# Turning the FFN input before its norm's root, and scaling each up piece by a row of roots on VectorE

## Chip, cores and metric

The kernel runs on one core of a Trainium2 chip. The metric is the device time of one execution in microseconds; lower is better.

## What is computed

The kernel is a two-layer encoder trunk over 256 tokens of width 1024. Each layer has an attention sublayer and then a gated MLP with a depthwise convolution of width 3 over the tokens. Only the MLP (the FFN) and the norm ahead of it are touched here:

```python
D_MODEL, SEQ, DEPTH, D_FF, CONV_WIDTH = 1024, 256, 2, 2816, 3

def rms_norm(x, g):
    y = x * lax.rsqrt(jnp.mean(x * x, axis=-1, keepdims=True) + NORM_EPS)
    return y * g

def conv_gated_mlp(h, w_up, conv_w, w_down):
    u = h @ w_up                                  # (tokens, 5632)
    up = jnp.pad(u, ((0, 0), (1, 1), (0, 0)))
    u = sum(up[:, t:t + S] * conv_w[t] for t in range(3))
    gate, val = jnp.split(u, 2, axis=-1)
    return (jax.nn.gelu(gate, approximate=True) * val) @ w_down

# in each layer, after the attention sublayer:
x = x + rms_norm(merged @ w_out, attn_post_norm)
h = rms_norm(x, ffn_pre_norm)
x = x + rms_norm(conv_gated_mlp(h, w_up, ffn_conv, w_down), ffn_post_norm)
```

## The kernel before

**Products in three passes.** Every large product is made of two rounded parts of each operand: a high part and a low part (`value - high`). `passes` (L1352) issues three matmuls for each 128-row step of the contraction: high by low, low by high, high by high (L1354 to L1356).

**Weights in pieces.** Weights come in pieces of at most 128x2048, in the order that `plan_pieces` writes out, through rings of 3 slots (`RING`). For each piece SP issues the DMA into `raw` when the low part of the piece three places earlier is done, ScalarE writes the high part (`split_hi`, L685 to L691), VectorE the low part (`split_lo`, L1030 to L1035), and TensorE uses it (`use_piece`, L1411). ScalarE may write a slot only when TensorE has finished the piece that held it (`piece_used`). Each engine walks the same list of steps (`STEPS`) in order. At step ("w", n) ScalarE and VectorE first split piece n + 2, then do what is due on piece n's result.

**The FFN.** It has NU = 11 units of 256 channels. For unit u there are two up pieces, number c = 2u (gate half) and c = 2u + 1 (value half), each 8 contraction steps by 2 channel blocks by 3 passes = 48 matmuls over 256 tokens, written into bank 4 + c % 4 with channels on partitions and tokens on the free axis. The down piece of unit u follows two units later (`LAG`), 24 matmuls of 512 columns. So the order is up 0 to up 5, down 0, up 6, up 7, down 1, and so on to up 20, up 21, down 8, down 9, down 10. On each up result:

- ScalarE multiplies the two blocks of the bank by the middle tap into `conv` (L930);
- VectorE adds the left tap and the right tap, two instructions each, reading the bank again (L1304, L1310);
- after the value half ScalarE takes Gelu of the gate half (L937), VectorE multiplies value by Gelu (L1316), ScalarE writes the high part of the product, `g_hi` (L942), and VectorE its low part, `g_lo` (L1318). The two wait for each other in turn. TensorE's down piece waits for `g_lo`.

**Between attention and FFN (the "mid" step, L854, L1231, L1669).** The output product `out` ends with a tile for each of the two token halves t. For each, ScalarE squares and sums the second 512 columns (`post_square`), GpSimd takes the root (`root`), VectorE multiplies by the gain and adds to `x` (`post_gained`, `post_add` L1187). Then the FFN's own norm follows: ScalarE squares `x` (`pre_square` L835), GpSimd takes the root, and VectorE writes `xn = x * root` (`pre_scale` L1073). TensorE turns `xn` by transposes (`turn_ffn` L1563), ScalarE writes the high part times the norm's gain (`ffn_hi` L803), VectorE the low part (`ffn_lo` L1062, in the order of `FFN_LO`), and up 0 begins. Between the two halves TensorE does `MID_WAIT` = 24 idle transposes (`keep_clock`, L1333).

Of the kernel before, what the change touches and what calls it, by code (L numbers as in the profile page):

```python
# [8 lines left out]
F32 = mybir.dt.float32  # L9
# [3 lines left out]
ALU = mybir.AluOpType  # L13
# [3 lines left out]
P = 128  # L17
# [27 lines left out]
MID_WAIT = 24  # L45
# [4 lines left out]
G_RING = 3  # L50
# [219 lines left out]
FFN_LO = [(0, 0), (0, 1), (1, 0), (1, 1), (0, 2), (1, 2), (0, 3), (1, 3)]  # L270
# [21 lines left out]
def build_trunk(nc, a, out):  # L292
    with ExitStack() as ctx:
# [73 lines left out]
        with ExitStack() as four:  # L367
# [3 lines left out]
            square_ffn = sb("square_ffn", [P, D], scope=four)  # L371
        with ExitStack() as six:
            sb("pad_six", [P, 5120], scope=six)
            par_rows = sb("par_rows", [44, 4 * DEPTH, P], scope=six)
# [40 lines left out]
        ffn_squares, xn_done = sem("ffn_squares"), sem("xn_done")  # L415
# [80 lines left out]
        def turned_bank(t, k):  # L496

            return bank[((0, 1, 6, 7), (2, 3, 0, 1))[t][k // 2]][:, (k % 2) * P:(k % 2 + 1) * P]
# [165 lines left out]
        def _(act):  # L664
# [150 lines left out]

            def pre_attn(l):
# [22 lines left out]
            for l in range(DEPTH):  # L839
                for step in STEPS:  # L840
# [13 lines left out]
                    elif what == "mid":  # L854
# [59 lines left out]
                    elif what == "w":  # L914
# [7 lines left out]
                        if kind == "up":  # L922
                            u, b = c // 2, c % 2
                            act.wait_ge(piece_used, l * NPIECE + (RING + n + 1))
                            if u >= 2:

                                act.wait_ge(g_lo_done, l * NU + (u - 1))
                            for j in range(2):
                                ch = 22 * b + 2 * u + j
                                last = nc.scalar.activation(conv[:, u % 2, b, j * SEQ:(j + 1) * SEQ],  # L930
                                                            bank[4 + c % 4][:, j * SEQ:(j + 1) * SEQ], ACT.Copy,
                                                            scale=par_all[:, l, 44 + ch:45 + ch])
                            last.then_inc(conv_mid, 1)
                            if c % 2 == 1:
# [3 lines left out]
                                act.wait_ge(g_ready, l * NU + (u + 1))  # L938
                                if u >= G_RING:

                                    act.wait_ge(piece_used, l * NPIECE + (RING + PIECES.index(("down", u - G_RING, 0, 2, 1024)) + 1))
                                nc.scalar.activation(by_class2(g_hi[:, u % G_RING, :]), own_order2(conv[:, u % 2, 1, :]), ACT.Copy).then_inc(g_hi_done, 1)  # L942
# [8 lines left out]
        def _(dve):  # L951
# [115 lines left out]
            def pre_scale(l, t):  # L1067
# [3 lines left out]
                for h in range(2):  # L1071
                    s = slice(h * 512, h * 512 + 512)
                    V.tensor_scalar(xn[:, t, s], x[:, t, s], roots[:, j:j + 1], None, ALU.mult).then_inc(xn_done, 1)  # L1073
# [675 lines left out]
```

## Time and profile before

| | |
|---|---|
| median of 3 runs | 1039.35 us (1038.99 to 1039.72) |
| the profiled execution | 1039.12 us |
| its span in the trace | 1037.0 us |
| TensorE matmul busy | 1015.7 us, 98% |
| VectorE busy | 658.0 us, 63% |
| ScalarE busy | 583.5 us, 56% |
| granted TensorE clock, mean | 0.998 |
| HBM traffic | 164 GB/s over the span |

The span is what the trace covers; 2.1 us of the profiled execution's time lie around it. Lines like L1062 are lines of the kernel before. The start of an interval is counted in microseconds from the start of the span. Where a row of the timeline says `[1.74 <-DVE x_normed L1073]`, the engine stood idle for 1.74 us before it, and what ended the idle time was that VectorE instruction.

### The profile page before, as it was taken

Reading aid. Unit: us, or ns where it says so; the run is one execution under the profiler, and the core shown is the slowest. Engines: PE = TensorE matmul, PEld = TensorE weight load, DVE = VectorE, ACT = ScalarE, POOL = GpSimd, SP = SyncE. Lnnn points to the kernel's source line nnn. Section 1 sums busy time; section 2 is a strip of 40 time slices with the busy share of each in tenths; the row PEclk is TensorE's granted clock in tenths of the full one; section 3 lists DMA queues with packets and bytes.
Section 4 is the critical chain, followed back from the end, with each engine's and each line's share of the span. In section 5 each row is a group of like instructions: output and inputs, shape, how many; then the busy total and the mean of one; then the engine's idle time right before and its main releaser. Section 6 shows DMA issues by size and latency. Waiting matters only on the chain.

```text
span 1037.0 us, 15899 instructions
## 1 busy us (share of the span) xinstructions
PE 1015.7 (98%) x6256; PEld 911.2 (88%) x6256; DVE 658.0 (63%) x886; ACT 583.5 (56%) x859; POOL 129.3 (12%) x257
## 2 busy tenths in 40 slices
PE   8999999999998999999999999999999989999997
PEld 7889999888877999999988899998888789999996
DVE  5636566655586776776765355656555878777675
ACT  5657666556445555454575666665553456545452
POOL 3353114000001000000024321220000010000000
PEclk9999999999999999999999999999999999999999
DMA  8555445444444654645455544465445444554541
GB/s 252 182 179 153 126 143 172 146 160 162 143 160 144 203 198 153 219 160 206 138 177 163 172 123 127 148 203 163 133 152 182 163 144 166 188 215 163 203 162 41
DMA packets 106222, 170.79 MB, mean 165 GB/s; under 512 B 3377, under 2 KB 72804, under 8 KB 106148
## 3 DMA queue, kind: packets, MB, share of 16 engines
q1 hardware_dynamic: 104860, 166.88, 48.8%
q10 hardware_dynamic: 1208, 2.63, 0.7%
q8 instruction: 50, 0.82, 0.3%
q0 software_dynamic: 80, 0.26, 0.1%
q14 instruction: 24, 0.20, 0.1%
HBM read 168.72 MB, written 1.05 MB: 164 GB/s over the span
## 4 chain that ended last, share of the span: by engine, by line
PE 92%; DVE 3%; DVEq 2%; ACT 1%; issue 1%; POOL 0%; POOLq 0%; ACTq 0%
PE bank L1354 27%; PE bank L1356 27%; PE bank L1355 27%; PE bank L1697 2%; PE bank L1598 1%; PE bank L1619 1%; DVEq L1206 1%; PE bank L1690 1%; DVE merged L1207 1%; PE bank L1607 1%; PE bank L1635 1%; PE bank L1642 1%; PE bank L1687 1%; DVE w_lo L1035 1%; PE bank L1649 1%
## 5 line engine op out<-in xcount | busy, mean ns | idle before, releaser
L1035 DVE TENSOR_TENSOR w_lo<-w_raw,w_hi 128x2048 fp32r<-128x2048 f32 (+3 forms) x174 | 363.0, 2097 | 189.8 <-ACT w_hi L691 189.6
L691 ACT ACTIVATE w_hi<-w_raw 128x2048 fp32r<-128x2048 f32 (+3 forms) x174 | 302.6, 1751 | 53.0 <-PE bank L1356 50.9
L1354 PE MATMUL bank<-w_hi,hT_lo 128*128 128x512 f32 (+2 forms) x700 | 258.4, 369 | 2.0 <-DVE hT_lo L1081 1.3
L1356 PE MATMUL bank<-w_hi,hT_hi 128*128 128x512 f32 (+2 forms) x700 | 252.9, 361 | 0.0
L1355 PE MATMUL bank<-w_lo,hT_hi 128*128 128x512 f32 (+2 forms) x700 | 252.5, 361 | 0.0
L1354 PE MATMUL bank<-hT_hi,w_lo 128*128 128x256 f32 x704 | 200.1, 284 | 1.7 <-DVE hT_lo L1062 1.6
L1356 PE MATMUL bank<-hT_hi,w_hi 128*128 128x256 f32 x704 | 199.7, 284 | 0.0
L1355 PE MATMUL bank<-hT_lo,w_hi 128*128 128x256 f32 x704 | 199.7, 284 | 0.0
L1354 PEld LDWEIGHTS bank<-w_hi,hT_lo 128*128 128x128 f32 x700 | 131.5, 188 | 18.2 <-issue 3.5
L1356 PEld LDWEIGHTS bank<-w_hi,hT_hi 128*128 128x128 f32 x700 | 131.4, 188 | 14.0
L1355 PEld LDWEIGHTS bank<-w_lo,hT_hi 128*128 128x128 f32 x700 | 131.6, 188 | 13.0
L1354 PEld LDWEIGHTS bank<-hT_hi,w_lo 128*128 128x128 f32 x704 | 135.7, 193 | 2.9 <-issue 2.0
L1355 PEld LDWEIGHTS bank<-hT_lo,w_hi 128*128 128x128 f32 x704 | 135.7, 193 | 0.6
L1356 PEld LDWEIGHTS bank<-hT_hi,w_hi 128*128 128x128 f32 x704 | 135.6, 193 | 0.0
L930 ACT ACTIVATE conv_out<-bank,par_all 128x256 f32<-128x256 f32 x88 | 36.8, 470 | 117.5 <-PE bank L1356 117.5
L601 POOL TENSOR_SCALAR mean_squares<-small 128x1 f32<-128x1 f32 x12 | 4.5, 375 | 610.5 <-ACT x_normed L828 603.8
L1304 DVE SCALAR_TENSOR_TENSOR conv_out<-bank,par_all,conv_out 128x255 f32<-128x255 f32 x88 | 38.4, 477 | 48.5 <-ACT conv_out L930 48.5
L1354 PE MATMUL bank<-w_hi,g_lo 128*128 128x512 f32 x176 | 68.7, 390 | 0.0
L1355 PE MATMUL bank<-w_lo,g_hi 128*128 128x512 f32 x176 | 68.7, 390 | 0.0
L1356 PE MATMUL bank<-w_hi,g_hi 128*128 128x512 f32 x176 | 68.5, 389 | 0.0
L942 ACT ACTIVATE g_hi<-conv_out 128x512 fp32r<-128x512 f32 x22 | 24.6, 1119 | 46.1 <-DVE conv_out L1316 46.1
L590 POOL TENSOR_TENSOR rope_a<-stage,cosT 128x96 f32<-128x96 f32 (+1 forms) x40 | 28.5, 712 | 162.9 <-ACT stage L710 136.2
(210 smaller groups left out, 1226.8 us busy)
## 6 DMA issues: line engine op xcount, KB each, us to landing
w_raw<-in_w_up_dram SPq DMA_DIRECT2D x44, 1024.0 KB, 5.0
w_raw<-in_w_in_dram SPq DMA_DIRECT2D x36, 1024.0 KB, 5.0
w_raw<-in_w_in_dram SPq DMA_DIRECT2D x36, 768.0 KB, 4.4
w_raw<-in_w_down_dram SPq DMA_DIRECT2D x22, 1024.0 KB, 5.1
w_raw<-in_w_out_dram SPq DMA_DIRECT2D x8, 1024.0 KB, 4.9
w_raw<-in_w_in_dram SPq DMA_DIRECT2D x8, 672.0 KB, 4.8
w_raw<-in_w_branch_mla_dram SPq DMA_DIRECT2D x4, 1024.0 KB, 4.9
w_raw<-in_w_branch_diff_dram SPq DMA_DIRECT2D x4, 1024.0 KB, 4.9
```

Source lines behind the costliest of these rows:

```text
L590: nc.gpsimd.tensor_tensor(ca, xr, c, ALU.mult)
L691: nc.scalar.activation(w_hi[:, n % RING, 0:nk * cols], raw[:, n % RING, 0:nk * cols], ACT.Copy).then_inc(hi_done, 1)
L930: last = nc.scalar.activation(conv[:, u % 2, b, j * SEQ:(j + 1) * SEQ], bank[4 + c % 4][:, j * SEQ:(j + 1) * SEQ], ACT.Copy, scale=par_all ...
L942: nc.scalar.activation(by_class2(g_hi[:, u % G_RING, :]), own_order2(conv[:, u % 2, 1, :]), ACT.Copy).then_inc(g_hi_done, 1)
L1035: V.tensor_tensor(w_lo[:, n % RING, s], raw[:, n % RING, s], w_hi[:, n % RING, s].bitcast(F32), ALU.subtract).then_inc(lo_done, 1)
L1206: dve.drain()
L1207: last = V.tensor_tensor(merged[:, t, s], merged[:, t, s], gs, ALU.add)
L1304: V.scalar_tensor_tensor(out=cv[:, o + 1:o + SEQ], in0=src[:, o:o + SEQ - 1], scalar=par_all[:, l, ch:ch + 1], in1=cv[:, o + 1:o + SEQ], o ...
L1354: PE.matmul(dst, lhs[1], rhs_hi, start=start, stop=False)
L1355: PE.matmul(dst, lhs[0], rhs_lo, start=False, stop=False)
L1356: return PE.matmul(dst, lhs[0], rhs_hi, start=False, stop=stop)
L1697: last = PE.transpose(T_BANK[:, b * P:(b + 1) * P], probs[:, i % 2, b * P:(b + 1) * P], ident[:])
```

## The change

- The transposes take `x` itself and wait for `x_ready`, so neither `xn` nor its root is needed ahead of them. `pre_scale` is gone. The squares of the second token half are moved behind the split of up 1 on ScalarE.
- VectorE fills two 128x128 tiles with the roots (`root_row`), TensorE multiplies them by the identity after up 0, which leaves in bank 3 a row of roots that is the same on all partitions, and VectorE copies it to `token_scale`.
- Every up result is multiplied by `token_scale` into a new SBUF buffer `up_scaled` of two slots (`scale_up`); the middle tap and both side taps read that buffer. TensorE's reuse of the bank waits for the multiply, no longer for the taps.
- Up 0 goes through its 8 contraction steps outermost, into two banks.
- The product of unit u is made one unit later and its low part another half unit later (`gated`, `gated_hi`, `gated_lo`). The last two units finish in the step of down 8, behind the split of down 10.
- `MID_WAIT` goes from 24 to 14, `G_RING` from 3 to 2, and `FFN_LO` takes both token halves of a pair of steps together.

Constants:

```diff
-MID_WAIT = 24
+MID_WAIT = 14
...
-G_RING = 3
+G_RING = 2
...
-FFN_LO = [(0, 0), (0, 1), (1, 0), (1, 1), (0, 2), (1, 2), (0, 3), (1, 3)]
+FFN_LO = [(t, pair) for pair in range(4) for t in range(NT)]
```

ScalarE, the mid step:

```diff
-                        ffn_hi(l, 0, (0, 1))
+                        ffn_hi(l, 0, range(4))
+                        ffn_hi(l, 1, range(4))
+                        split_hi(l, UP0 + 1)
                         pre_square(l, 1)
-                        ffn_hi(l, 0, (2, 3))
-                        ffn_hi(l, 1, range(4))
                         act.dma_start(post_gain[:], a["ffn_post_norm"][l, :].partition_broadcast(P)).then_inc(gain_landed, 16)
-                        split_hi(l, UP0 + 1)
```

ScalarE, the step of an up piece, and of down 8:

```diff
-                            act.wait_ge(piece_used, l * NPIECE + (RING + n + 1))
-                            if u >= 2:
+                            act.wait_ge(up_scaled_done, l * 2 * NU + (c + 1))
+                            if b == 1 and u >= 2:
...
-                                last = nc.scalar.activation(conv[:, u % 2, b, j * SEQ:(j + 1) * SEQ],
-                                                            bank[4 + c % 4][:, j * SEQ:(j + 1) * SEQ], ACT.Copy,
+                                last = nc.scalar.activation(conv[:, u % 2, b, j * SEQ:(j + 1) * SEQ], up_scaled[:, c % 2, j, :], ACT.Copy,
...
+                                if u:
+                                    gated_hi(l, u - 1)
+                        elif kind == "down" and c == NU - 1 - LAG:
+                            gated_hi(l, NU - 1)
```

VectorE's new functions:

```diff
+            def root_row(l, t):
...
+                V.tensor_scalar(root_rows[:, t, :], ident[:], 0.0, roots[:, j:j + 1], ALU.mult, ALU.add).then_inc(root_rows_ready, 1)
+            def scale_rows(l):
+                dve.wait_ge(scales_full, l + 1)
+                for t in range(NT):
+                    V.tensor_copy(tile_tokens(token_scale, t), bank[3][:, t * P:(t + 1) * P].rearrange("p (h j) -> p j h", h=2))
+                dve.drain()
+            def scale_up(l, n, c):
+                dve.wait_ge(piece_used, l * NPIECE + (RING + n + 1))
+                if c == 0:
+                    scale_rows(l)
+                    for j in range(2):
+                        last = V.tensor_tensor(up_scaled[:, c % 2, j, :], up_half(c, j), token_scale, ALU.mult)
+                else:
+                    last = V.tensor_tensor(up_scaled[:, c % 2, :, :], bank[4 + c % 4][:].rearrange("p (j q) -> p j q", j=2),
+                                           token_scale.rearrange("p (o q) -> p o q", o=1).broadcast_to([P, 2, SEQ]), ALU.mult)
+                last.then_inc(up_scaled_done, 1)
+            def gated(l, u):
+                dve.wait_ge(gelu_done, l * NU + (u + 1))
+                V.tensor_tensor(conv[:, u % 2, 1, :], conv[:, u % 2, 1, :], conv[:, u % 2, 0, :], ALU.mult).then_inc(g_ready, 1)
+            def gated_lo(l, u):
+                dve.wait_ge(g_hi_done, l * NU + (u + 1))
+                V.tensor_tensor(by_class2(g_lo[:, u % G_RING, :]), own_order2(conv[:, u % 2, 1, :]),
+                                by_class2(g_hi[:, u % G_RING, :].bitcast(F32)), ALU.subtract).then_inc(g_lo_done, 1)
```

VectorE, the mid step, the step of an up piece and that of down 8, each of the last two behind the split of piece n + 2:

```diff
+                        root_row(l, 0)
                         split_lo(l, UP0 + 1)
+                        root_row(l, 1)
...
+                            scale_up(l, n, c)
+                            if b == 0 and u >= 2:
+                                gated_lo(l, u - 2)
+                            if b == 1 and u >= 1:
+                                gated(l, u - 1)
                             dve.wait_ge(conv_mid, l * 2 * NU + (c + 1))
+                            dve.drain()
...
+                        elif kind == "down" and c == NU - 1 - LAG:
+                            gated_lo(l, NU - 2)
+                            dve.drain()
+                            gated(l, NU - 1)
+                            dve.drain()
+                            gated_lo(l, NU - 1)
```

TensorE, the up pieces and `turn_ffn`:

```diff
-                        pe.wait_ge(conv_done, BASE + l * 2 * NU + (c - 3))
...
+                        pe.wait_ge(up_scaled_done, l * 2 * NU + (c - 3))
+                    order = [(k, j) for k in range(8) for j in range(2)] if c == 0 else [(k, j) for j in range(2) for k in range(8)]
...
+                    if c == 0:
+                        last.then_inc(piece_used, 1)
+                        pe.wait_ge(root_rows_ready, l * NT + NT)
+                        for t in range(NT):
+                            last = PE.matmul(bank[3][:, t * P:(t + 1) * P], root_rows[:, t, :], ident[:], start=True, stop=True)
+                        last.then_inc(scales_full, 1)
+                        return
...
-                        pe.wait_ge(xn_done, l * 4 + (2 * t + k // 4 + 1))
+                        pe.wait_ge(x_ready, l * 8 + (X_START + 2 * t + k // 4 + 1))
-                    last = PE.transpose(turned_bank(t, k), xn[:, t, k * P:(k + 1) * P], ident[:])
+                    last = PE.transpose(turned_bank(t, k), x[:, t, k * P:(k + 1) * P], ident[:])
```

## Rows read from the trace of the kernel before

**Rows 1.** Page, part 1: busy us (share of the span) xinstructions of two engines

```profile
PE 1015.7 (98%) x6256; PEld 911.2 (88%) x6256; DVE 658.0 (63%) x886; ACT 583.5 (56%) x859; POOL 129.3 (12%) x257
```

**Rows 2.** Windows, TensorE: stretch, its us, busy (xstarts), granted clock, DMA share, GB/s

```profile
325.04:332.67 7.63, 4.76 (x42) 0.97 0.00 0
332.67:339.92 7.25, 7.25 (x50) 0.80 0.33 111
835.26:842.88 7.62, 4.76 (x42) 1.00 0.00 0
842.88:849.22 6.34, 6.28 (x50) 1.00 0.32 91
```

**Rows 3.** Chain that ended last, layer 0, out to up 0: start, us, what

```profile
325.08 0.70 ACT x_normed L828 x2
...
326.88 0.76 DVE x_rows L1187
327.66 1.40 ACT x_normed L835 x4
...
329.56 0.58 POOL roots L606
330.16 0.50 DVE x_normed L1073
...
331.24 0.64 ACT hT_hi L803 x2
331.91 0.62 DVE hT_lo L1062 x2
...
332.67 0.55 PE bank L1354
```

**Rows 4.** Timeline of the same stretch: start, us, engine, line, instruction, xcount, [idle before]

```profile
325.82 1.15 ACT L803 ACTIVATE hT_hi<-bank,par_all 128x128 fp32r<-128x128 f32 x4
...
326.28 2.78 PE L1333 MATMUL bank<-ident 128*128 128x128 f32 x24
...
330.80 1.06 PE L1563 MATMUL bank<-ident,x_normed 128*128 128x128 f32 x8 [1.74 <-DVE x_normed L1073]
...
331.91 3.20 DVE L1062 SCALAR_TENSOR_TENSOR hT_lo<-bank,par_all,hT_hi 128x128 fp32r<-128x128 f32 x12 [0.86 <-ACT hT_hi L803]
```

**Rows 5.** Timeline of ScalarE in layer 0's FFN: its start, and its end

```profile
346.58 1.28 ACT L937 ACT_TABLE_LOAD   x1
...
487.62 0.84 ACT L930 ACTIVATE conv_out<-bank,par_all 128x256 f32<-128x256 f32 x2 [3.12 <-PE bank L1356]
...
492.15 3.71 ACT L691 ACTIVATE w_hi<-w_raw 128x2048 fp32r<-128x2048 f32 x2
498.84 0.84 ACT L930 ACTIVATE conv_out<-bank,par_all 128x256 f32<-128x256 f32 x2 [2.98 <-PE bank L1356]
...
504.60 0.84 ACT L930 ACTIVATE conv_out<-bank,par_all 128x256 f32<-128x256 f32 x2 [3.12 <-PE bank L1356]
```

**Rows 6.** Groups by line and shape, VectorE: xcount | busy us, mean ns | idle before

```profile
L1035 DVE TENSOR_TENSOR w_lo<-w_raw,w_hi 128x2048 fp32r<-128x2048 f32 x120 | 273.2, 2291 | 98.3 <-ACT w_hi L691 98.1
L1310 DVE SCALAR_TENSOR_TENSOR conv_out<-bank,par_all,conv_out 128x255 f32<-128x255 f32 x88 | 38.4, 478 | 3.3
...
L1318 DVE TENSOR_TENSOR g_lo<-conv_out,g_hi 128x512 fp32r<-128x512 f32 x22 | 24.3, 1102 | 26.1 <-ACT g_hi L942 26.1
...
L1175 DVE TENSOR_TENSOR merged<-bank,post_gain 128x512 f32<-128x512 f32 x8 | 5.5, 690 | 5.6 <-ACT x_normed L828 5.6
...
L1126 DVE SCALAR_TENSOR_TENSOR probs<-probs,small 128x256 f32<-128x256 f32 x16 | 7.6, 516 | 0.6
```

**Rows 7.** The same view, ScalarE

```profile
L691 ACT ACTIVATE w_hi<-w_raw 128x2048 fp32r<-128x2048 f32 x120 | 227.4, 1910 | 39.7 <-PE bank L1356 37.5 <-DMA w_raw<-in_w_in_dram 2.2
...
L942 ACT ACTIVATE g_hi<-conv_out 128x512 fp32r<-128x512 f32 x22 | 24.6, 1119 | 46.1 <-DVE conv_out L1316 46.1
...
L937 ACT ACTIVATE conv_out<-conv_out 128x512 f32<-128x512 f32 x22 | 13.9, 631 | 0.0
```

More of the change, by code:

```diff
@@ L371, in build_trunk @@
             square_ffn = sb("square_ffn", [P, D], scope=four)
+            up_scaled = sb("up_scaled", [P, 2, 2, SEQ], scope=four)
         with ExitStack() as six:
@@ L496, in turned_bank, with up_half @@
         def turned_bank(t, k):
-            return bank[((0, 1, 6, 7), (2, 3, 0, 1))[t][k // 2]][:, (k % 2) * P:(k % 2 + 1) * P]
+            return bank[((0, 1, 6, 7), (2, 3, 5, 0))[t][k // 2]][:, (k % 2) * P:(k % 2 + 1) * P]
+        def up_half(c, j):
+            if c == 0:
+                return bank[(4, 2)[j]][:, 0:SEQ]
+            return bank[4 + c % 4][:, j * SEQ:(j + 1) * SEQ]
+        root_rows = xn[:, 0, 0:NT * P].rearrange("p (t q) -> p t q", t=NT)
+        token_scale = xn[:, 0, 512:512 + SEQ]
         def tile_tokens(cols, t):
@@ L814, in begin_hi, with gated_hi @@
                     last.then_inc(turn_hi, 1)
+            def gated_hi(l, u):
+                act.wait_ge(g_ready, l * NU + (u + 1))
+                if u >= G_RING:
+                    act.wait_ge(piece_used, l * NPIECE + (RING + PIECES.index(("down", u - G_RING, 0, 2, 1024)) + 1))
+                nc.scalar.activation(by_class2(g_hi[:, u % G_RING, :]), own_order2(conv[:, u % 2, 1, :]), ACT.Copy).then_inc(g_hi_done, 1)
             def pre_attn(l):
@@ L1425, in use_piece @@
                     if c >= 4:
-                        pe.wait_ge(conv_done, BASE + l * 2 * NU + (c - 3))
-                    for j in range(2):
-                        for k in range(8):
-                            if c == 0 and j == 0 and k % 2 == 0:
-                                last_of = max(FFN_LO.index((t, k // 2)) for t in range(NT))
-                                pe.wait_ge(turn_emptied, l * NTURN + (TURN_BEFORE["ffn"] + last_of + 1))
-                            last = passes(bank[4 + c % 4][:, j * SEQ:(j + 1) * SEQ],
-                                          (hi[:, k, j * P:(j + 1) * P], lo[:, k, j * P:(j + 1) * P]),
-                                          hT_hi[:, k, :], hT_lo[:, k, :], k == 0, k == 7)
+                        pe.wait_ge(up_scaled_done, l * 2 * NU + (c - 3))
+                    order = [(k, j) for k in range(8) for j in range(2)] if c == 0 else [(k, j) for j in range(2) for k in range(8)]
+                    for k, j in order:
+                        if c == 0 and j == 0 and k % 2 == 0:
+                            last_of = max(FFN_LO.index((t, k // 2)) for t in range(NT))
+                            pe.wait_ge(turn_emptied, l * NTURN + (TURN_BEFORE["ffn"] + last_of + 1))
+                        last = passes(up_half(c, j), (hi[:, k, j * P:(j + 1) * P], lo[:, k, j * P:(j + 1) * P]),
+                                      hT_hi[:, k, :], hT_lo[:, k, :], k == 0, k == 7)
+                    if c == 0:
+                        last.then_inc(piece_used, 1)
[4 more added lines that the diff above has]
+                        return
                     last.then_inc(piece_used, 1)
```

32 lines of the change are left out of this document (7 added, 25 removed).

## Prediction

> **What bounds the kernel now.** I read the page first, then the windows of the two stretches that the change aims at, then the chain of waits and the timeline inside them. The page says that TensorE is busy for 1015.7 of 1037.0 us [rows 1]: it sets the time, and only where it stands still or runs at a low clock can anything be won. VectorE (658.0 us) and ScalarE (583.5 us) have room over the whole kernel, but that is an average. The windows show where TensorE stands: from the end of the output product to up 0 it passes 7.63 us in layer 0 and 7.62 us in layer 1, 4.76 us of them busy [rows 2], and most of that busy time is the 24 idle transposes (2.78 us) and the 16 real ones [rows 4]. Up 0 itself takes 7.25 us in layer 0, at a mean clock of 0.80, and 6.34 us in layer 1 at the full clock [rows 2]. The chain shows what fills the stretch: squares of the last tile at 325.08, VectorE's add into x at 326.88, then the second norm (ScalarE squares at 327.66, GpSimd's root at 329.56, VectorE's scaling at 330.16), then transposes, a high part at 331.24, a low part at 331.91, and up 0 at 332.67 [rows 3]. Inside the FFN, ScalarE still waits about 3 us for TensorE before each up result, so VectorE and ScalarE are ahead there [rows 5].
>
> From the starts 498.84 and 504.60 an up piece takes TensorE 5.76 us at the full clock, and from 487.62 to 498.84 one down and one up take 11.22, so a down piece takes 5.46 [rows 5].
>
> **Part 1, ahead of up 0: the second norm leaves the chain.** x's first half is done at 326.88 + 0.76 = 327.64 [rows 3]. The link from VectorE to the ScalarE high part is taken from the chain: scaling begins at 330.16 and takes 0.50, and the high part begins at 331.24, so 0.58 after the source is ready; the low part begins 0.67 after the high part, and lasts 0.62; up 0 begins 0.14 after it [rows 3]. The high parts of the first token half must be out of the way: they can start at 325.82, as now, and eight at 0.28 (four took 1.15 [rows 4]) end at 328.06, in time. VectorE is at its two adds until 328.3 and does one low-part pair of the first half (0.56) until about 328.8. So: high part at 328.22, low part at 328.89 to 329.51, up 0 at 329.65. That is 3.0 us earlier, in each layer. Of 14 idle transposes at 0.116 (24 took 2.78 [rows 4]) the last ends near 327.6, before the data is there, so cutting ten of them is needed for this gain and none is late.
>
> Up 0 then takes 5.76 if nothing holds it. The low parts of a contraction pair of both halves take 4 x 0.267 = 1.07 us (twelve took 3.20 [rows 4]); with the steps outermost TensorE needs 12 x 0.12 = 1.44 us for such a pair, so it is not held. In layer 0 the low clock came after TensorE had stood for 1.74 us ahead of the transposes [rows 4] and again ahead of up 0; both idle times shrink below 0.5 us, so I take the full clock. Out end to up 0 end: before 7.63 + 7.25 = 14.88 and 7.62 + 6.34 = 13.96 [rows 2]; after 4.61 + 5.76 = 10.37. **Gain 4.5 + 3.6 = 8.1 us.**
>
> **Part 2, after up 0: the row of roots.** Two matmuls of 128 columns: like two transposes at 0.13 (eight took 1.06 [rows 4]), 0.25 us. Is TensorE held by VectorE's second root row? VectorE ends its low parts at 328.89 + 14 x 0.267 = 332.65; then a root row of 128 columns (0.2 to 0.27, as such a low part), the low part of up 1, 2.29 [rows 6], to 335.14, and the second root row to 335.30. The second root itself: squares after the split of up 1 on ScalarE, which ends its high parts at 330.4 and the split at 332.2, and 2.5 us from squares to root (327.66 to 330.14 [rows 3]), so 334.7. Up 0 ends at 335.41: the row is held by nothing, with 0.1 us to spare. **Loss 0.25 us per layer.**
>
> **Part 3, VectorE in the first up pieces, which have no down pieces between them.** Prices: scaling 0.69 (the same shape from a bank, 690 ns [rows 6]). The tap instructions now have both tensor inputs in SBUF. The row of that kind that is nearest is 516 ns against 478 ns for a tap today [rows 6]; I take 0.95 us for two instead of 0.87. ScalarE's two middle taps from SBUF I take at 0.90 instead of 0.84 [rows 5]. An engine starts its next instruction some 0.1 us before the visible end of the last. Now VectorE, late from the start:
> - low part of up 2 to 337.74, two copies of 128 columns 0.50, scaling of up 0 in two halves 0.94 (0.27 and 0.48 each, as the low parts and taps of these widths), to 339.16; ScalarE to 340.09; four taps to 342.09.
> - piece 1: low part of up 3 to 344.28, scaling 344.88, ScalarE 345.81, taps 347.81. ScalarE has a table load (1.28 [rows 5]), Gelu 0.63 and the split of up 4, 1.91 [rows 7], to 349.54, and VectorE waits for it.
> - piece 2: 2.20 + 0.69 + 0.93 + 1.90, to 355.29. Piece 3: low part and scaling to 358.18; on ScalarE taps 0.78, Gelu 0.53, g_hi 1.02, split of down 0 1.91, to 362.45; VectorE's low part of down 0 to 364.77, scaling of piece 4, then at last g_lo of unit 0 (1.10 [rows 6]) to 366.38.
>
> TensorE ends up 5 at 335.66 + 5 x 5.76 = 364.46 and can begin down 0 at 366.5: it **waits 2.1 us per layer**. The same lateness brings up 7's low part of the weights 0.2 us late. Ends: nothing, if scaling and taps come 0.15 us cheaper each and the queues keep up; 3.8 us if scaling costs 1.0 instead of 0.69. From down 1 on, each unit has a down piece of 5.46 us in which VectorE's only new work is one split, and it catches up: per unit of 16.98 us it has 3 x 2.25 + 2 x 0.69 + 4 x 0.95 + 0.69 + 1.10 = 13.7 us. Scaling then hides, and g_lo of unit u - 2, half a piece ahead of down u - 2, is some 4 us early.
>
> **Part 4, the last units.** Down 9 needs g_lo of unit 9, and that is now queued in the step of down 8, behind the split of down 10, whose two halves wait for one another and with them everything behind them on VectorE. Count from the end of up 21: start 0.1, scaling and handing over 0.72, ScalarE's middle taps 0.78, Gelu 0.53, g_hi of unit 9 1.02, then the split of down 10 1.91, VectorE's low part of down 10 0.03 + 2.20, g_lo 1.10, to TensorE 0.13. Together 8.5 us, and down 8 covers 5.46 of it: **TensorE waits 3.1 us per layer.** Before, g_lo of unit 9 was long done. Down 10 is not held: product, g_hi and g_lo of unit 10 need 0.69 + 1.12 + 1.10 and some 0.1, less than the 5.46 of down 9. The next layer's first splits and the last squares keep their distance to the end of down 10. The durations of this chain have their rows [rows 5 to 7]; its ends are 2.8 and 3.7 us.
>
> This idle time is longer than the 1.74 us after which the clock fell in layer 0, and did not fall in layer 1 [rows 2, 4]. What a spell at 1.2 GHz costs: up 0 took 7.25 us at a mean clock of 0.80, of which 0.20 x 7.25 = 1.45 are the lost clock, and 0.9 more than in layer 1 at 1.00 [rows 2]. I take one such spell in the two layers at 1.4 us; ends 0 and 2.9.
>
> **The sum.** -8.1 + 2 x (0.25 + 2.1 + 0.2 + 3.1) = +3.2 us, with a clock spell +4.6. Against the profiled execution's own 1039.12 (its 1037.0 us of span and 2.1 around it) that is 1043.7; the median of the runs is 0.23 above it, so 1043.9.
>
> One rule bears on the taps. The Trainium skill ("VectorE: DVE Perf Modes", section on the TRN2 errata) has VectorE's fixed cost with an SBUF source at 58 cycles and with a PSUM source at 120, so moving the source to SBUF would make a tap about 0.06 us cheaper, not dearer. The rows that are nearest here say the contrary, 516 against 478 ns [rows 6]. By the page each layer would end some 0.4 us earlier and the sum would be 3.8 instead of 4.6; by the rows it is as above.
>
> **Rivals.**
> - *Only the last unit waits.* If scaling costs less than its nearest row or the queues slip past one another, down 0 doesn't wait: -8.1 + 2 x (0.25 + 3.1) = -1.4, 1038.0; halfway there, and without a clock spell, 1040 to 1041. For it: VectorE's and ScalarE's lateness of 2 us in part 3 is the end of a long chain of small terms. Against: the same queue without the scaling already runs a pair of pieces in more than 11.52 us at the start of the FFN. Chance 0.2 for a time within 0.2% (1037.3 to 1041.4), about what a measurement of this kernel can tell from no change.
> - *The postponed products cost nothing* (faster). Only the gain and the broadcast stay: -7.6, 1031.8. It needs g_lo of unit 9 within 5.46 us of up 21's end, against the 8.5 counted; all that comes below 1037.3 has chance 0.1.
> - *VectorE becomes the bound of the FFN* (slower still). It decides when a scaling with its drain costs over 1 us: then a unit's work nears 14.5 us plus waits for ScalarE, down 0 waits 3.6 and down 9 3.7, and the sum is 9.4 with a spell, 1048.8. Chance 0.05.
> - *The norm leaves the chain but something else holds up 0*, ScalarE's eight high parts or the clock: up to 1 us less gain per layer, 1045.9. Chance 0.1, also slower.
>
> My forecast, slower by some 2 to 7 us, has 0.55 and with the last two rivals slower has 0.7, same 0.2, faster 0.1. The range 1039.8 to 1046.5 leaves out 0.12 below and 0.08 above.
>
> **What would show it.** Right: up 0 begins 4.6 us after the output product ends; up 0 takes about 5.8 us in both layers; a wait of TensorE for g_lo of about 2 us ahead of down 0 and of about 3 us ahead of down 9, in both layers; none between. In VectorE's timeline the last split of 2048 columns stands ahead of the last two low parts. Wrong: no idle time of TensorE ahead of down 9 (part 4 misread), scaling well off 0.69, taps at or below 478 ns, or a high part ahead of up 0 that waits for ScalarE.

## The result, and the profile after

The changed kernel takes 1047.68 us in the median of four executions (1045.8 to 1050.25), beside 1039.53 us for the kernel before (1038.99 to 1040.34). The ratio is 1.0079, with a 95% interval of 1.0057 to 1.0102: slower by 0.8%. The profiled execution took 1045.8 us, with a span of 1044.0. The page of the kernel after answers to [rows 1]:

```profile
PE 1017.9 (97%) x6244; PEld 911.3 (87%) x6244; DVE 681.8 (65%) x932; ACT 586.7 (56%) x859; POOL 132.4 (13%) x257
```

TensorE is busy for 2.2 us longer and stands still for 4.8 us longer. The windows of the kernel after answer to [rows 2], with the stretch ahead of down 9 added (columns: stretch, its us, busy time of PE, PEld, DVE, ACT and POOL, granted clock, DMA share, GB/s):

```profile
324.90:329.50 4.60, 3.85 (x31) 3.02 (x29) 3.38 (x8) 4.19 (x16) 0.76 (x2) 1.00 0.00 0
329.50:335.48 5.98, 5.98 (x48) 5.78 (x48) 5.35 (x14) 5.58 (x9) 2.44 (x3) 1.00 0.29 90
...
508.70:511.70 3.00, 0.00 (x1) 0.04 (x1) 2.91 (x3) 0.00 (x0) 0.00 (x0) 1.00 0.00 1
...
838.88:843.47 4.59, 3.84 (x30) 3.01 (x29) 3.38 (x8) 4.18 (x16) 0.76 (x2) 1.00 0.00 0
843.47:849.30 5.83, 5.83 (x48) 5.78 (x48) 5.35 (x14) 5.58 (x9) 2.37 (x2) 1.00 0.25 93
```

From the output product to up 0 it is now 4.60 and 4.59 us instead of 7.63 and 7.62, and up 0 runs at the full clock in both layers. That is the gain, and it came. Three idle times of TensorE in layer 0's FFN, from its timeline, say where more than that was spent (start, us, engine, line, instruction; in brackets the idle time before it and what ended it):

```profile
336.36 0.71 PE L1487 MATMUL bank<-ident,x_normed 128*128 128x128 f32 x4 [0.88 <-DVE x_normed L1087]
...
367.03 0.47 PE L1401 MATMUL bank<-w_hi,g_lo 128*128 128x512 f32 x1 [1.17 <-issue]
...
511.70 0.47 PE L1401 MATMUL bank<-w_hi,g_lo 128*128 128x512 f32 x1 [3.00 <-DVE g_lo L1116]
```

The first is the matmul of the row of roots, the second is down 0, the third is down 9. Layer 1 has the same three: 0.87, 1.54 and 2.99 us. The profile names no releaser for the second (`issue`), but VectorE's low part of unit 0 ends at 366.93, 0.10 us before down 0 starts:

```profile
365.87 1.06 DVE L1116 TENSOR_TENSOR g_lo<-conv_out,g_hi 128x512 fp32r<-128x512 f32 x1
```

Stretch by stretch, in layer 0 (layer 1 in brackets), from the starts of TensorE's pieces in the timeline of both kernels:

| stretch | before | after | predicted |
|---|---|---|---|
| out end to up 0 | 7.63 (7.62) | 4.60 (4.59) | 4.61 |
| up 0 to down 0 | 35.89 (34.98) | 37.53 (37.90) | 36.85 |
| down 0 to down 8 | 135.84 (135.84) | 136.04 (136.06) | 136.04 |
| down 8 to down 9 | 5.47 (5.47) | 8.63 (8.61) | 8.56 |
| down 9 to the end of down 10 | 11.04 (11.04) | 12.75 (11.17) | 11.04, and 1.4 once |

The durations that the prediction had to bound, in the groups by line and shape, VectorE first:

```profile
L1358 DVE SCALAR_TENSOR_TENSOR conv_out<-up_scaled,par_all,conv_out 128x255 f32<-128x255 f32 x88 | 38.7, 482 | 3.3
...
L1104 DVE TENSOR_TENSOR up_scaled<-bank,x_normed 128x512 f32<-128x512 f32 x42 | 29.0, 690 | 17.4 <-PE bank L1403 17.4
```

```profile
L948 ACT ACTIVATE conv_out<-up_scaled,par_all 128x256 f32<-128x256 f32 x88 | 40.2, 504 | 155.6 <-DVE up_scaled L1104 145.9 <-DVE up_scaled L1102 9.7
```

**The row of roots.** The prediction had the second root ready at 334.7. GpSimd's timeline of the kernel after shows it 1.3 us later:

```profile
332.75 2.18 POOL L612 TENSOR_SCALAR mean_squares<-small 128x1 f32<-128x1 f32 x1 [6.05 <-ACT x_normed L854]
335.08 0.19 POOL L615 TENSOR_TENSOR mean_squares<-mean_squares,small 128x1 f32<-128x1 f32 x1
335.41 0.57 POOL L617 TENSOR_TENSOR roots<-mean_squares,minus_half 128x1 f32<-128x1 f32 x1
```

and VectorE's, of the same stretch, what ran beside it:

```profile
332.56 2.29 DVE L1051 TENSOR_TENSOR w_lo<-w_raw,w_hi 128x2048 fp32r<-128x2048 f32 x1
336.02 0.28 DVE L1087 TENSOR_SCALAR x_normed<-ident,roots 128x128 f32<-128x128 f32 x1 [1.17 <-POOL roots L617]
```

The first GpSimd line, L612, adds a constant to one number per partition. It took 2.18 us, began 0.19 us after VectorE's split and ended 0.08 us after it. In layer 1 it took 2.17 us. The steps that follow it on GpSimd, VectorE's root row and TensorE's two small matmuls all hang on it, so up 1 starts at 336.82, where without a hold it would follow the last up 0 matmul (335.20) at 335.32: 1.50 us instead of 0.25.

**Down 9.** VectorE's timeline, from the end of up 21:

```profile
508.28 2.29 DVE L1051 TENSOR_TENSOR w_lo<-w_raw,w_hi 128x2048 fp32r<-128x2048 f32 x1 [1.44 <-ACT w_hi L702]
510.49 1.06 DVE L1116 TENSOR_TENSOR g_lo<-conv_out,g_hi 128x512 fp32r<-128x512 f32 x1
511.64 0.69 DVE L1111 TENSOR_TENSOR conv_out<-conv_out 128x512 f32<-128x512 f32 x1
```

and ScalarE's:

```profile
505.34 1.11 ACT L833 ACTIVATE g_hi<-conv_out 128x512 fp32r<-128x512 f32 x1
506.35 1.90 ACT L702 ACTIVATE w_hi<-w_raw 128x2048 fp32r<-128x2048 f32 x1
```

The high part of unit 9 ends at 506.45. Its low part could follow, while VectorE stands idle for 1.44 us; but the split of down 10 is ahead of it in VectorE's queue and waits for ScalarE's half. After the wait of 3.00 us the clock fell, in layer 0 only (windows of TensorE: stretch, us, busy, clock, DMA share, GB/s):

```profile
512.00:513.00 1.00, 1.00 (x4) 0.63 0.84 234
513.00:514.00 1.00, 1.00 (x4) 0.50 1.05 388
514.00:515.00 1.00, 1.00 (x4) 0.50 0.10 34
515.00:516.00 1.00, 1.00 (x4) 0.67 0.08 16
...
1026.10:1027.10 1.00, 1.00 (x5) 1.00 0.00 0
```

0.50 is the lower of the two levels, 1.2 GHz. The lost clock in the four windows is 0.37 + 0.50 + 0.50 + 0.33 = 1.7 us. From its start to that of down 10, down 9 takes 7.15 us in layer 0 and 5.57 in layer 1, so one spell at the lower level costs about 1.6 us of time.

### The profile page after: what moved, and what is told of

Same layout as the page of the kernel before. It is cut to its first block, busy times and chain, and to the rows that moved or that the text cites. A ratio compares the mean times of both kernels' runs of the same rounds, so it can differ in the third digit from the quotient of the medians.

```text
span 1044.0 us, 15933 instructions
## 1 busy us (share of the span) xinstructions
PE 1017.9 (97%) x6244; PEld 911.3 (87%) x6244; DVE 681.8 (65%) x932; ACT 586.7 (56%) x859; POOL 132.4 (13%) x257
## 4 chain that ended last, share of the span: by engine, by line
PE 88%; DVE 4%; ACT 3%; DVEq 2%; issue 1%; POOL 1%; POOLq 0%; ACTq 0%
PE bank L1401 26%; PE bank L1403 26%; PE bank L1402 25%; PE bank L1751 2%; DVE w_lo L1051 1%; PE bank L1652 1%; PE bank L1673 1%; DVEq L1250 1%; ACT w_hi L702 1%; PE bank L1744 1%; DVE merged L1251 1%; PE bank L1661 1%; PE bank L1689 1%; PE bank L1696 1%; PE bank L1741 1%
## 5 line engine op out<-in xcount | busy, mean ns | idle before, releaser
L948 ACT ACTIVATE conv_out<-up_scaled,par_all 128x256 f32<-128x256 f32 x88 | 40.2, 504 | 155.6 <-DVE up_scaled L1104 145.9
L612 POOL TENSOR_SCALAR mean_squares<-small 128x1 f32<-128x1 f32 x12 | 7.8, 654 | 614.4 <-ACT x_normed L847 598.9
L1352 DVE SCALAR_TENSOR_TENSOR conv_out<-up_scaled,par_all,conv_out 128x255 f32<-128x255 f32 x88 | 38.7, 481 | 16.9 <-ACT conv_out L948 15.3
L1401 PEld LDWEIGHTS bank<-w_hi,g_lo 128*128 128x128 f32 x176 | 33.5, 190 | 16.3 <-issue 9.8
```

Source lines behind the costliest of these rows:

```text
L1352: V.scalar_tensor_tensor(out=cv[:, o + 1:o + SEQ], in0=src[:, o:o + SEQ - 1], scalar=par_all[:, l, ch:ch + 1], in1=cv[:, o + 1:o + SEQ], o ...
L1401: PE.matmul(dst, lhs[1], rhs_hi, start=start, stop=False)
```

## The experiments

The theory: the split of down 10 queued ahead of unit 9's low part costs 3 us per layer and the clock after it; VectorE's split shuts GpSimd out, which costs the row of roots 1.2 us per layer; a chain of small delays at the start of the FFN costs the wait ahead of down 0. The main rivals: that the scaling or the postponement as such is what costs, that it is the 14 idle transposes, and that GpSimd's long step has to do with the kernel's position or its own queue rather than with VectorE. The runs of the kernel before on the same chips had medians of 1039.46 (the first four experiments) and 1039.18 us (the others), beside 1039.53 in the comparison above; the change itself was not run again beside them, so differences from its 1047.68 of a few tenths of a us say nothing.

**Only the low part of unit 9 ahead of the split.**

```diff
+                        if kind == "down" and c == NU - 1 - LAG:
+                            gated_lo(l, NU - 2)
+                            dve.drain()
                         if n + 2 < NPIECE and n not in (OUT0 - 1, UP0 - 1) and (l == 0 or n):
                             split_lo(l, n + 2)
...
                         elif kind == "down" and c == NU - 1 - LAG:
-                            gated_lo(l, NU - 2)
-                            dve.drain()
                             gated(l, NU - 1)
```

> The changed kernel with one edit: in the step of down 8, VectorE writes the low part of unit 9 ahead of the split of down 10 instead of behind it. Theory: the 3.0 us for which TensorE stands ahead of down 9 is only this place in VectorE's queue; g_hi of unit 9 ends 3.3 us after up 21 and VectorE's taps 3.7, so the low part is there at 4.8, ahead of the 5.5 at which down 8 ends. The wait goes in both layers, -6.0 us, and with it the spell at 1.2 GHz behind it, -1.6 each time there was one: about 1038.5 to 1040, a profile without a gap ahead of down 9. Rival: the lateness comes from ScalarE or VectorE being late as a whole, then down 10 is late instead (split of down 10 behind the products) and less than 2 us go.

1037.92 us (1037.51 to 1039.16, ten executions), ratio to the kernel before 0.9986, 95% interval 0.9977 to 0.9996. TensorE doesn't wait ahead of down 9 in either layer. VectorE's timeline of this kernel:

```profile
506.76 1.09 DVE L1116 TENSOR_TENSOR g_lo<-conv_out,g_hi 128x512 fp32r<-128x512 f32 x1
508.30 2.29 DVE L1051 TENSOR_TENSOR w_lo<-w_raw,w_hi 128x2048 fp32r<-128x2048 f32 x1 [0.44 <-ACT w_hi L702]
```

The low part sits in the idle time, and the split of down 10 ends as it did. The order of two instructions was worth 9.8 us between the medians: down 9 starts 5.47 us after down 8 in both layers instead of 8.63 and 8.61, which is 6.3, and the rest, 3.5, is about what the clock takes back (below, 3.3). With it alone the change is a small gain, 0.14%.

**Only the second root early.** On ScalarE the squares of the second half go ahead of the split of up 1, on VectorE both root rows go ahead of it.

```diff
-                        split_hi(l, UP0 + 1)
                         pre_square(l, 1)
+                        split_hi(l, UP0 + 1)
...
-                        split_lo(l, UP0 + 1)
                         root_row(l, 1)
+                        split_lo(l, UP0 + 1)
```

> The changed kernel with the second half's squares ahead of the split of up 1 on ScalarE and both root rows ahead of that split on VectorE. Theory: GpSimd's first step of the second root took 2.18 us instead of 0.22 because it fell into VectorE's split, an instruction with both inputs in SBUF, and ran only when that was over; squares earlier, it falls under the low parts, which read PSUM and one SBUF tensor, and takes 0.2 to 0.5 again. TensorE's wait behind up 0 falls from 1.3 to at most 0.4 us, some of it goes back ahead of down 0 (+0.4): -0.8 per layer, -1.6 in all. Rival: GpSimd's step is slow there whatever VectorE does (2 us again), or held by low parts too; then the root row comes at about the same time after the squares as now, 4.1 us from the squares' start, and TensorE gains less than 0.5.

1046.26 us (1044.96 to 1047.81, four executions), ratio 1.0067, 1.0052 to 1.0082: 1.4 less than the change's median, about the 1.6 of the theory, though the two intervals overlap; what is certain is in the trace. GpSimd's timeline:

```profile
331.88 0.22 POOL L612 TENSOR_SCALAR mean_squares<-small 128x1 f32<-128x1 f32 x1 [4.25 <-ACT x_normed L854]
332.57 0.19 POOL L615 TENSOR_TENSOR mean_squares<-mean_squares,small 128x1 f32<-128x1 f32 x1 [0.47 <-ACT x_normed L854]
332.90 0.60 POOL L617 TENSOR_TENSOR roots<-mean_squares,minus_half 128x1 f32<-128x1 f32 x1
```

L612 takes 0.22 us again, beside VectorE's low parts (L1078), which read one operand from a bank. TensorE no longer waits behind up 0: up 1 starts 6.20 us after up 0 instead of 7.32. So of the 1.50 us counted above, 1.12 are the hold, and 0.38 is what the row of roots costs when nothing holds it. But the idle time ahead of down 0 grows from 1.17 to 1.60 us: part of what the hold cost had been covered, since VectorE, late with unit 0's low part, used the time that TensorE lost. From up 0 to down 0 it is now 36.83 us (37.19 in layer 1) instead of 37.53 (37.90), so the hold cost 0.7 us per layer net, 1.4 in all.

**The low part a half step earlier, and the root early.** The low part of unit u - 1 is made at the end of the step of the value half instead of in the next gate half; for the last unit the product is made there as well.

```diff
-                            if b == 0 and u >= 2:
-                                gated_lo(l, u - 2)
...
+                            if b == 1 and u >= 1:
+                                gated_lo(l, u - 1)
+                            if b == 1 and u == NU - 1:
+                                dve.drain()
+                                gated(l, u)
                         elif kind == "down" and c == NU - 1 - LAG:
-                            gated_lo(l, NU - 2)
-                            dve.drain()
-                            gated(l, NU - 1)
-                            dve.drain()
                             gated_lo(l, NU - 1)
```

> The second edit and another place for the low part: at the end of each value half's step, where VectorE now waits 1.46 us for the split, and the last product there too. Theory: takes the waits ahead of down 0 and down 9 away, but VectorE's and ScalarE's lateness of the first six pieces then shows ahead of up 7 (low part of its weights), 1.4 us. Per layer 193.8 us from the output product's end to down 10's end, against 199.5 and 198.3 now and 195.9 and 194.9 before: 1035.5 to 1037.5, faster than before by 2 to 4 us. Rival: moving the low part makes VectorE late in every unit, gaps of TensorE in the units 3 to 10, slower than before.

1036.20 us (1035.94 to 1036.93, six executions), ratio 0.9972, 0.9960 to 0.9983. The waits ahead of down 0 and down 9 are gone; in each layer's FFN one is left, ahead of up 7, where VectorE's split is late (1.23 us in layer 1; here layer 0):

```profile
378.13 0.39 PE L1400 MATMUL bank<-hT_hi,w_lo 128*128 128x256 f32 x1 [1.24 <-DVE w_lo L1051]
```

**The clock kept up.** 24 idle transposes into a bank that is free stand ahead of the wait of down 9. They leave the 3 us in place and give TensorE something to do in them.

```diff
+                    if c == NU - 2:
+                        keep_clock(24, bank[6][:, 0:P])
```

> The changed kernel with 24 transposes of the identity into an idle bank between down 8 and down 9, 2.8 us of work that fits into the 3.0 us for which TensorE stands there. Nothing waits for them. Theory: the executions between 1045.8 and 1050.3 us differ in how often the clock fell behind the long waits, 1.6 us each time; with the wait filled the clock stays at 2.4 GHz, all executions come to 1044 to 1045.5 and lie within 1 us of one another. Rival: the spread is from elsewhere (DMA, start of the kernel); then it stays, the median stays near 1047.5, or it grows by the transposes that run late.

1044.37 us (1044.31 to 1044.71, four executions), ratio 1.0049, 1.0032 to 1.0066. TensorE's timeline of the place:

```profile
508.81 2.78 PE L1380 MATMUL bank<-ident 128*128 128x128 f32 x24
511.90 0.50 PE L1401 MATMUL bank<-w_hi,g_lo 128*128 128x512 f32 x1 [0.32 <-DVE g_lo L1116]
```

Down 9 starts 8.57 us after down 8, against 8.63 without the edit, and the clock stays at 1.00 behind it. That alone is 3.3 us from median to median, and the four executions lie within 0.4 us of each other instead of 4.5. So the median execution of the change loses about two spells of 1.6 us, not one, and nearly all of its spread is whether the clock falls. Two other profiled executions with the same wait, those of the probe and of 24 idle transposes (both below), bear this out: each has a spell in both layers. Down 9 in the two layers of the probe's execution (windows of TensorE: stretch, us, busy, clock, DMA share, GB/s):

```profile
511.97:519.03 7.06, 7.06 (x24) 0.77 0.50 136
1026.16:1033.31 7.15, 7.15 (x25) 0.76 0.01 2
```

The slowest execution of the change, 1050.25 us, has more than two spells explain; it was not profiled. In the second experiment's profile the clock fell once behind a wait of 1.97 us, ahead of down 0 of layer 1, so down 9 need not be the only place.

**A probe of GpSimd.** 120 one-column additions that nothing needs, one after the other, in layer 0's FFN; nothing else waits for them.

```diff
+                if l == 0:
+                    for _ in range(120):
+                        nc.gpsimd.tensor_scalar(small[:, 60:61], half[:], EPS, None, ALU.add)
+                        pool.drain()
```

> The changed kernel with 120 more GpSimd steps in layer 0 behind the second root, each one column from SBUF to SBUF (half to an unused column of small) and a drain, nothing waits for them. They run beside the first units of the FFN and meet every kind of VectorE instruction. Theory: GpSimd stands while VectorE runs an instruction with two SBUF inputs (weight split, product, low part of a product, side taps that now read up_scaled and conv), so a step that falls into a split of 2.29 us takes up to that, and steps beside a scaling (one input in PSUM) or in idle time take 0.2 us. Rival: GpSimd's durations are scattered without regard to what VectorE runs.

1047.48 us in one execution. The probe lets one instruction be seen beside each kind of VectorE instruction. GpSimd:

```profile
336.79 2.04 POOL L672 TENSOR_SCALAR small<-half 128x1 f32<-128x1 f32 x1 [0.15 <-issue]
338.98 0.21 POOL L672 TENSOR_SCALAR small<-half 128x1 f32<-128x1 f32 x1 [0.15 <-issue]
339.34 0.21 POOL L672 TENSOR_SCALAR small<-half 128x1 f32<-128x1 f32 x1 [0.15 <-issue]
...
341.16 0.42 POOL L672 TENSOR_SCALAR small<-half 128x1 f32<-128x1 f32 x1 [0.15 <-issue]
...
343.08 2.05 POOL L672 TENSOR_SCALAR small<-half 128x1 f32<-128x1 f32 x1 [0.15 <-issue]
```

VectorE:

```profile
336.47 2.28 DVE L1055 TENSOR_TENSOR w_lo<-w_raw,w_hi 128x2048 fp32r<-128x2048 f32 x1
...
339.23 0.76 DVE L1106 TENSOR_TENSOR up_scaled<-bank,x_normed 128x256 f32<-128x256 f32 x2
...
341.02 0.88 DVE L1356 SCALAR_TENSOR_TENSOR conv_out<-up_scaled,par_all,conv_out 128x255 f32<-128x255 f32 x2 [1.04 <-ACT conv_out L952]
...
342.78 2.28 DVE L1055 TENSOR_TENSOR w_lo<-w_raw,w_hi 128x2048 fp32r<-128x2048 f32 x1
```

Beside the scaling, which reads a bank, and in VectorE's idle time the addition takes 0.21 us. Beside a tap, a product, the low part of a product or a split, whose tensor inputs both lie in SBUF, it lasts until that instruction is over: 0.39 to 0.48, 0.68 (at 358.95), 1.02 to 1.13 and 2.03 to 2.17 us. It isn't the position and not the queue. VectorE's own times are what they were (a split takes 2292 ns in the mean in both kernels): it doesn't pay, GpSimd does.

Two tensors in SBUF are not the only case. The kernel before already had the pattern in this very stretch, under a VectorE instruction that reads one tensor and a column of roots from SBUF (L1073); a step beside a low part that reads a bank (L1062) took 0.22 us:

```profile
324.79 0.52 POOL L601 TENSOR_SCALAR mean_squares<-small 128x1 f32<-128x1 f32 x1
...
328.47 0.22 POOL L601 TENSOR_SCALAR mean_squares<-small 128x1 f32<-128x1 f32 x1 [1.63 <-ACT x_normed L835]
```

```profile
324.74 0.88 DVE L1073 TENSOR_SCALAR x_normed<-x_rows,roots 128x512 f32<-128x512 f32 x2 [1.87 <-POOL roots L606]
...
328.21 1.12 DVE L1062 SCALAR_TENSOR_TENSOR hT_lo<-bank,par_all,hT_hi 128x128 fp32r<-128x128 f32 x4
```

**The scaling without the postponement.** Product, high part and low part are made in the step of their own value half, as in the kernel before, with three slots of `g_hi` and `g_lo`.

```diff
-G_RING = 2
+G_RING = 3
...
+                            if b == 1:
+                                dve.drain()
+                                gated(l, u)
+                                gated_lo(l, u)
```

(The calls of `gated`, `gated_hi` and `gated_lo` in the later steps are gone, and ScalarE's `gated_hi(l, u)` follows the Gelu.)

> The scaling without the postponement: product, high part and low part of a unit are made in its own value half's step, as before, in a ring of 3. Theory: the postponement fills VectorE's waits for ScalarE; without it VectorE needs a table's worth more per unit (waits for the middle taps, Gelu and g_hi open up again), so it runs late in the first six pieces by some 5 us more: gaps of TensorE ahead of down 0 and up 7 of about 3.6 us each, small ones of 0.3 later, none ahead of down 9: per layer 203.8 us instead of 199.5, 1053 to 1056. Rival: the postponement is what costs, so this comes out below 1045.

1059.28 us (1058.66 to 1060.33, four executions), ratio 1.0194, 1.0179 to 1.0209, 3.3 us above the upper end of what I expected. Its list of what TensorE waits for (engine, line, waited for: us in total, times, longest):

```profile
PE bank L1392 <- DVE w_lo L1048: 16.2, 21, 3.5
```

VectorE's splits are late 21 times, 10 of them in the FFN of each layer: by 3.48 us ahead of down 0, by 2.1 ahead of up 7, by about 0.24 in each of the seven units that follow, and by 0.5 ahead of down 10. The two long ones are no longer than the 3.6 us that I expected of each. What lies above the expectation is the clock again: behind the wait of 3.48 us, down 0 takes 7.23 us to the start of up 6 in layer 0 and 7.20 in layer 1, instead of 5.55 in the change, 1.7 us in each layer. So the rival that the postponement is what costs is false: between the medians it is worth 11.6 us, and what costs 3 us per layer is its tail, the place of unit 9's low part.

**24 idle transposes again.**

```diff
-MID_WAIT = 14
+MID_WAIT = 24
```

> The changed kernel with 24 idle transposes between the turned halves again, not 14. Theory: they last 1.16 us longer and the transposes of the second half, ready 0.33 us after the 14 end, begin 0.83 us later in each layer; up 0 begins later by that, but its end is followed by the wait for the root row, 0.9 us, which takes the lateness in: less than 0.5 us slower in all, 1047 to 1048.5. Rival: a longer run of transposes keeps the clock and gains.

1047.87 us (1046.79 to 1048.71, four executions), ratio 1.0080, 1.0063 to 1.0097: no difference from the change's 1047.68 that the medians can tell. The trace can. Its windows from the output product's end to up 0, and from there to down 0:

```profile
325.28:330.45 5.17, 4.37 (x41) 1.00 0.00 0
330.45:367.99 37.54, 35.48 (x293) 1.00 0.48 157
```

Up 0 starts 5.17 us after the output product ends, 0.57 later than with 14, and the stretch from there to down 0 is 37.54 us, as in the change (37.53). In layer 1 it is 5.17 and 37.86, against 4.59 and 37.90. So the lateness is not taken in: the wait for the row of roots stays at 0.88 us, because ScalarE's squares of the second half stand behind the high parts of the turned data and start 0.57 us later themselves (7.57 us after the output product's end, against 7.00). The ten transposes cost 1.1 us in the two layers, and my theory that the wait hides them is wrong; in the medians the spells of the clock cover a difference of this size.

**All of it, and the table load out of the chain.** The kernel of the third experiment, and a Gelu of one column on ScalarE ahead of its wait for up 0, so that the load of the Gelu table falls into idle time.

```diff
+                            if c == 0:
+                                nc.scalar.activation(table_seed[:], table_seed[:], ACT.Gelu_apprx_tanh)
                             act.wait_ge(up_scaled_done, l * 2 * NU + (c + 1))
```

> The low part at the end of the value half's step, the root ahead of the split of up 1, and one more edit: ScalarE takes a Gelu of one column behind the split of up 2, where it stands idle for 4.7 us, so that the table load (1.28 us) is over before the middle taps of up 1. Theory: the load sat in the chain of the late queue (VectorE waited 1.85 us for the split of up 4); with it out, TensorE's wait ahead of up 7 falls from about 1.4 to 0.5 us: 192.4 us per layer, 1.4 us less than without the edit: 1033.5 to 1035. Rival: the queue is late for VectorE's own work and the load was beside it; then no change against the kernel without this edit (1036.2).

1033.24 us (1033.15 to 1033.35, four executions), ratio 0.9943, 0.9928 to 0.9957. It beats both kernels: 14.4 us below the change and 5.9 below the kernel before. ScalarE's timeline:

```profile
335.36 1.28 ACT L943 ACT_TABLE_LOAD   x1
336.65 0.20 ACT L943 ACTIVATE table_seed<-table_seed 128x1 f32<-128x1 f32 x1
339.32 0.91 ACT L950 ACTIVATE conv_out<-up_scaled,par_all 128x256 f32<-128x256 f32 x2 [2.46 <-DVE up_scaled L1104]
```

The load of 1.28 us is over 2.7 us before ScalarE has up 0 to work on. What is left of the wait ahead of up 7 in layer 0 is 0.24 us, and the layer's stretch from out to down 10 takes 192.5 us instead of 195.9 before and 199.6 after the change:

```profile
376.44 0.39 PE L1402 MATMUL bank<-hT_hi,w_lo 128*128 128x256 f32 x1 [0.24 <-DVE w_lo L1053]
```

The gain over the third experiment is 3.0 us between the medians; by the traces the same stretch falls from 194.0 to 192.5 us, 1.5 per layer, about one table load each. As the scaling is in this kernel too, the scaling as such isn't what made the change slow.

## Why the prediction was right in sign and short in size

The prediction said 1043.9, with a range to 1046.5; it is 1047.68. The sign was right, and so were the waits ahead of down 0 and down 9; the size was 3.8 us short. Two terms failed: the row of roots, taken as held by nothing (1.4 us in the two layers), and the clock, taken as one spell of 1.4 us (it costs 3.3 in the median).

- **Part 1 was right.** 4.60 us from out end to up 0 was counted as 4.61, and up 0 had the full clock in both layers. Its matmuls pass in 5.82 us from the first to the next possible start, counted as 5.76. The seventh experiment bears out that the ten idle transposes had to go for that start: with them up 0 starts 0.57 us later in each layer, and down 0 as much later.
- **Part 2 is the step that failed: the row "held by nothing, with 0.1 us to spare".** Up 1 starts 1.50 us after it could have followed up 0, in each layer, instead of 0.25; by the second experiment 1.12 of it is the hold and 0.38 the row itself. The two and a half microseconds "from squares to root" came from [rows 3], where GpSimd's steps ran beside a VectorE that was idle or reading banks (at 328.47 it is 0.22 us beside L1062). The change moves the same steps under VectorE's split, whose inputs both lie in SBUF, and there a step of 0.22 us takes 2.18. The Trainium skill has this rule: "SBUF — State Buffer", section on SBUF's two separate sides, says that VectorE and GpSimd share one pair of ports, which a VectorE instruction with two SBUF inputs holds against a reading GpSimd instruction until it is done. The trace agrees, by 2.18 us under a split of 2.29, and the prediction should have weighed it: the split was named in the same paragraph as the root. With no slack in a sum, each of its terms has to be read at its new neighbours.
- **Part 3 was right in mechanism, and in size once the row of roots is not held.** Down 0 waited 1.17 and 1.54 us (1.33 and 1.70 from start to start), not the 2.0 to 2.1 counted. Without the hold, in the second experiment, it is 1.76 and 2.12 from start to start. So of the 0.7 us that layer 0's wait fell short, 0.4 is TensorE's own lateness from the row of roots. VectorE's `g_lo` of unit 0 was ready at 366.93, against the 366.38 that were counted. The scaling takes 690 ns, exactly its nearest row. The taps take 482 ns, neither the 516 that I took from the nearest SBUF row nor about 0.42: from SBUF and from a bank they cost the same within 4 ns [rows 6]. The second of these prices was the one by the Trainium skill ("VectorE: DVE Perf Modes", section on the TRN2 errata), and no row here bears it out; the same section adds that its 58 cycles are too few and that about 150 were measured, which the prediction left out. ScalarE's middle taps take 0.91 us a pair, counted 0.90. The errors of parts 2 and 3 overlap, and together they leave up 0 to down 0 at 37.53 and 37.90 us instead of 36.85: 1.7 us too little in the two layers, 1.4 of them the hold.
- **Part 4 was right**: 3.00 and 2.99 us ahead of down 9, counted 3.1, in both layers, for the reason given. The first experiment takes it away by moving that one low part.
- **The clock was a term that was mis-sized.** One spell at 1.4 us was counted for the two layers. The profiled execution had one, of 1.6; but it is the fastest of the four, the profiled executions of the probe and of the seventh experiment had two each (1047.48 and 1048.71 us), and by the fourth experiment the spells cost 3.3 us in the median. That is 1.9 us more than counted, and above the term's upper end of 2.9. Either error alone would have stayed within the range; together they didn't.

1.7 for the row of roots and down 0, and 1.9 for the clock, are 3.6 of the 3.8 us. The rest is within what the medians can tell. Of the rivals, "only the last unit waits" and "VectorE becomes the bound" are wrong for this kernel: from down 1 to down 8 TensorE never waits, and 136.04 us from down 0 to down 8 are 0.2 more than before, the 0.2 that was counted for up 7. "The postponed products cost nothing" fails by the wait ahead of down 9, and "something else holds up 0" by up 0's start and clock. (The sum of the rival "VectorE becomes the bound" is 8.8 by its own terms, 1048.2, and not 9.4.)

## What to carry to other kernels

When work is postponed in an in-order queue, write out the queue's last steps by hand: what is due in the last step must not stand behind an instruction that waits for another engine. When a chain is moved to another place, price each small step of it by what will run beside it there, and above all a GpSimd step by whether VectorE reads two SBUF operands at that time. In this kernel an idle time of some 3 us of TensorE cost more than itself, and not in every execution, so its upper price, one spell for each such wait, belongs into the range. And where medians can't tell a small difference, compare the same stretch in two traces.

## What the runs showed of the hardware

- A GpSimd instruction on one column takes 0.21 us alone or beside a VectorE instruction that reads a bank. It lasts as long as the VectorE instruction beside it when that one has two tensor inputs in SBUF: 0.4 to 0.5 under a tap, 0.68 under a product of 512 columns, 1.0 to 1.1 under the low part of a product, 2.03 to 2.18 us under a split of 2048. Under a multiply of 512 columns by a column of roots, all in SBUF, it takes 0.52. VectorE isn't slowed.
- Behind a wait of 3.0 us the granted clock fell to 0.50 in layer 0 and stayed at 1.00 in layer 1 of one execution, and fell in both layers of two others. Each spell costs 1.5 to 1.6 us. The same program so spreads over 4.5 us; with the wait filled by 24 transposes it spreads over 0.4 us.
- A scalar-tensor-tensor of 255 columns takes 482 ns with both tensors in SBUF and 478 with one in a bank; ScalarE's multiplying copy of 256 columns takes 504 ns from SBUF and 470 from a bank, by the groups of the two kernels (the pair 0.91 instead of 0.84 [rows 5]).
- The load of the Gelu table takes 1.28 us once per layer, and moved out of the chain it gave 1.5 us per layer.
